# Sliding-window attention in bands on 32-row tiles, its probabilities turned by VectorE, in a two-layer float32 trunk

## The reference, cut to what matters

```python
q, k, v, z = jnp.split(x @ w_in, [SWA_Q, SWA_Q + SWA_KV, SWA_Q + 2 * SWA_KV], axis=-1)
q, k = _rope(q, pos), _rope(k, pos)                 # 16 and 2 heads of 64
s = jnp.einsum("bnqhgd,bnkhd->bnhgqk", qb, kb).astype(f32) * HD ** -0.5   # blocks of 128 queries, 256 keys
rel = qi + W - kj
valid = (rel >= 0) & (rel < W) & (blk * W + kj - W >= 0)
s = jnp.where(valid[None, :, None, None], s, -jnp.inf)
p = jax.nn.softmax(jnp.concatenate([s, sink], axis=-1), axis=-1)[..., :-1]
o = jnp.einsum("bnhgqk,bnkhd->bnqhgd", p.astype(vb.dtype), vb).reshape(bsz, t_len, SWA_Q)
return (o * jax.nn.silu(z)) @ w_out
```

## Time and profile before

| | |
|---|---|
| median of 3 runs | 1020.15 us (1019.94 to 1022.01) |
| the profiled execution | 1020.63 us |
| its span, first to last instruction | 1018.9 us |
| its mean granted TensorE clock | 0.998 of full speed |
| the stage of the change, first to last gate group but one | 768.85 to 909.99 us of the span |

### The profile page before, as it was taken

One profiled execution on the slowest core, in us unless ns is written; L12 is line 12 of the kernel. 1 busy time (PEld: TensorE's weight loads), 2 busy tenths in 40 slices (PEclk: granted clock), 3 DMA queues, 4 the chain that ended last, 5 costly groups with the idle time before them and its releaser, 6 DMA issues.

```text
span 1018.9 us, 17445 instructions
## 1 busy us (share of the span) xinstructions
PE 993.9 (98%) x6318; PEld 813.1 (80%) x6318; DVE 675.4 (66%) x1296; ACT 462.2 (45%) x1349; POOL 291.7 (29%) x647
## 2 busy tenths in 40 slices
PE   7999999999999999999999999999999999999997
PEld 6888787888788787888888888888787777776885
DVE  4677768586867676754456766533447888788655
ACT  4655466575756666644355111302126545556000
POOL 1008483828474746563000000000102222221000
PEclk9999999999999999999999999999999999999999
DMA  6232414133241324234113212302000010014211
GB/s 211 64 104 68 119 42 110 52 67 96 42 120 37 114 47 106 55 87 115 42 41 144 85 42 65 102 11 73 1 21 22 22 43 21 23 63 115 93 42 62
DMA packets 89974, 71.04 MB, mean 70 GB/s; under 512 B 32768, under 2 KB 79008, under 8 KB 89888
## 3 DMA queue, kind: packets, MB, share of 16 engines
q1 hardware_dynamic: 55568, 53.07, 17.4%
q10 hardware_dynamic: 34320, 16.84, 6.6%
HBM read 59.38 MB, written 10.52 MB: 69 GB/s over the span
## 4 chain that ended last, share of the span: by engine, by line
PE 82%; DVE 7%; ACT 6%; DMA 3%; issue 2%; ACTq 0%; DVEq 0%
PE ps L741 28%; PE ps L928 14%; PE ps L1000 9%; PE ps L1105 8%; PE ps L1130 3%; PE ps L941 2%; PE ps L1089 2%; DVE tok L1524 2%; PE ps L1117 2%; PE ps L898 1%; PE ps L909 1%; DMA ws_raw<-in_b_w_in 1%; PE ps L907 1%; PE ps L818 1%; PE ps L886 1%
## 5 line engine op out<-in xcount | busy, mean ns | idle before, releaser
L741 PE MATMUL ps<-act_hi,w_hi 128*128 128x512 f32 x512 | 223.6, 437 | 0.2 <-DVE w_lo L1475 0.2
L741 PE MATMUL ps<-act_hi,w_lo 128*128 128x512 f32 x512 | 201.1, 393 | 0.0
L741 PE MATMUL ps<-act_lo,w_hi 128*128 128x512 f32 x512 | 200.2, 391 | 0.0
L1524 DVE SCALAR_TENSOR_TENSOR tok<-xs,convw,tok 128x512 f32<-128x512 f32 x144 | 115.9, 805 | 15.5 <-ACT xs L1236 13.7
L672 POOL TENSOR_TENSOR rank<-inverse,tok 128x60 f32<-128x60 f32 (+24 forms) x248 | 98.2, 396 | 96.2 <-DMA tok<-blocks_in 78.0
L741 PEld LDWEIGHTS ps<-act_hi,w_lo 128*128 128x128 f32 x512 | 96.1, 188 | 21.2
L741 PEld LDWEIGHTS ps<-act_hi,w_hi 128*128 128x128 f32 x512 | 97.0, 189 | 12.2 <-issue 0.4
L741 PEld LDWEIGHTS ps<-act_lo,w_hi 128*128 128x128 f32 x512 | 97.2, 190 | 10.0
L675 POOL TENSOR_TENSOR inverse<-inverse,rank 128x60 f32<-128x60 f32 (+24 forms) x248 | 97.5, 393 | 19.4
L928 PE MATMUL ps<-wo_hi,act_hi 128*128 128x512 f32 x224 | 88.4, 395 | 1.0 <-DVE wo_lo L1627 1.0
L928 PE MATMUL ps<-wo_lo,act_hi 128*128 128x512 f32 x224 | 87.5, 391 | 0.0
(11 more groups left out here) (273 smaller groups left out, 2187.0 us busy)
## 6 DMA issues: line engine op xcount, KB each, us to landing
w_raw<-in_a_w_in ACTq DMA_DIRECT2D x32, 512.0 KB, 4.3
tok<-in_x SPq DMA_DIRECT2D x8, 512.0 KB, 7.1
decay<-gc_rows SPq DMA_DIRECT2D x8, 512.0 KB, 5.5
tok<-blocks_in SPq DMA_DIRECT2D x32, 128.0 KB, 2.6
v_turn<-v_tok SPq DMA_DIRECT2D x8, 512.0 KB, 6.0
v_tok<-v_turn SPq DMA_DIRECT2D x32, 128.0 KB, 2.9
xres<-in_x SPq DMA_DIRECT2D x8, 512.0 KB, 3.6
ws_raw<-in_b_w_in SPq DMA_DIRECT2D x16, 256.0 KB, 2.7
```

The costliest lines, as they stand in the source:

```text
L741: mm = pe.matmul(ps[:, g % 2, :], lhs[:, k, :], rhs[:, k, HALF * b:HALF * (b + 1)], start=(i == 0), stop=(i == GROUP - 1))
L1524: ins = dve.scalar_tensor_tensor(conv[b], xs[:, b, k:k + HALF], convw[:, k, tile:tile + 1], conv[b], ALU.mult, ALU.add)
```

## The change

A quarter of a block, 32 queries, can see only 159 keys, and these lie in five aligned blocks of 32. The new kernel works on that band (`BAND` = 5, `WIDE` = 160 columns):

- `logits` makes 16 matmuls for each unit, of 160 columns, on eight tiles of 64x32, so that each quarter's queries have their band at column 0. The scale of the logits moves into the copy of the turned queries (L1416).
- The mask touches only the first and the last block of the band (`edges`, 256 elements). The sink is column 161, copied there in every fourth pair; the maximum goes over 161 columns and comes out negated, and the exponentials take the sink along. The operations at L1851, L1854, L1860 and L1429 fall away.
- DVE only inverts the sum (`inverted`). The multiplication by it, over 640 elements, is POOL's, and so is `low_gate`, in every second pair. POOL's selections fall away.
- DVE turns the probabilities by one transpose of 32x32 blocks for each unit (`turned`, 640 elements) straight into `prob`. PE's transposes and ACT's copies of them fall away.
- `values` makes 40 matmuls for each unit (20 in the first block of queries), of 64 columns, on eight tiles of 32x64. Their contraction is over 32 keys, so each quarter needs v in its own 32 partitions: `v_rows`, filled four times over (2 MB) from a copy in DRAM. Three quarters come out in banks 5 to 7, taken by DVE in two operations of 192 elements (`branch`), the fourth in a bank of logits, taken by ACT (`last_rows`).
- The logits of a pair's second unit come a third of a gate group later than the first's.
- At the end of the stage DVE turns the last two units and takes pair 14 ahead of `low_wo(1, 1)`.

```diff
@@ PE
+            def logits(v):
+                k, x, jj, n = unit(v)
+                if k:
+                    pe.wait_ge(s_e, place(k - 1, x) + 1)
+                if k >= 2 and v % 2:
+                    pe.wait_ge(s_ob3, k - 1)
+                for b in range(2):
+                    for a in range(4):
+                        at = n * P + 32 * a
+                        for e in range(2):
+                            r = 64 * e
+                            mm = pe.matmul(ps[32 * a:32 * a + 32, 1 + 2 * x + e, 256 * b:256 * b + WIDE],
+                                           bT[r:r + 64, 2 * jj + b, at:at + 32], kd[r:r + 64, jj // 2, at:at + WIDE],
+                                           start=True, stop=True)
                 mm.then_inc(s_s, 1)
...
+            def values(v):
+                k, x, jj, n = unit(v)
                 kv = jj // 2
...
+                pe.wait_ge(s_pt, v + 1)
+                if v == 0:
+                    pe.wait_ge(s_vr, 64)
+                if v % 2 == 0:
+                    pe.wait_ge(s_e, min(v + 3, UNITS))
+                    if k:
+                        pe.wait_ge(s_ob, 2 * k)
+                for i in range(BAND):
+                    for a in range(4):
+                        row = 4 * (n - 1) + a + i
+                        if row < 0:
+                            continue
+                        bank = last_rows_bank(k) if a == 3 else VALUE_BANK + a
+                        for e in range(2):
+                            mm = pe.matmul(ps[64 * e:64 * e + 64, bank, 64 * x:64 * x + 64],
+                                           v_rows[32 * a:32 * a + 32, row, 64 * kv:64 * kv + 64],
+                                           prob[32 * a:32 * a + 32, x, i, 2 * e:2 * e + 2, :].rearrange("p h q -> p (h q)"),
+                                           start=(i == 0 or row == 0), stop=(i == BAND - 1))
...
             for k in range(PAIRS - 1):
-                turn_probs(2 * k)
-                turn_probs(2 * k + 1)
-                for third in range(3):
-                    project_gate(k + 1, third)
+                project_gate(k + 1, 0)
+                logits(2 * k + 3)
+                project_gate(k + 1, 1)
+                project_gate(k + 1, 2)
                 values(2 * k)
                 values(2 * k + 1)
                 if k + 2 < PAIRS:
                     logits(2 * k + 4)
-                    logits(2 * k + 5)
...
+            pe.wait_ge(s_e, UNITS)
+            pe.wait_ge(s_ob3, PAIRS - 1)
             out_step(1, 0, 0)
-            pe.wait_ge(s_e, UNITS)
             out_step(1, 1, 0)
             values(UNITS - 2)
@@ POOL
+            for v in range(UNITS):
+                k, x, jj, n = unit(v)
+                probs = logit[k % 2][x][:, :, 0:WIDE]
+                pool.wait_ge(s_rden, v + 1)
+                pool.tensor_tensor(probs, probs, sm["rden"][:, k % 2, x, :].unsqueeze(2).broadcast_to([P, 4, WIDE]),
+                                   ALU.mult).then_inc(s_norm, 1)
+                if v % 4 == 0 and v // 4 + 1 < NK:
+                    low_gate(v // 4 + 1)
@@ SP
+            sp.wait_ge(q_val, NT)
+            sp.dma_start(v_rows_out.rearrange("t p d -> p t d"), vv[:, :, :]).then_inc(s_vd, 16)
             for j in range(NK):
                 if j:
                     sp.wait_ge(z_los, j)
+                if j == 2:
+                    sp.wait_ge(s_vd, 16)
+                    sp.wait_ge(q_group, 3 * NT)
+                    for a in range(4):
+                        sp.dma_start(v_rows[32 * a:32 * a + 32, :, :],
+                                     v_rows_out.rearrange("t (b i) d -> i (t b) d", b=4)).then_inc(s_vr, 16)
                 sp.dma_start(z_raw[:, :, :], wb_tiles[:, :, SWA_Z0 + P * j:SWA_Z0 + P * (j + 1)]).then_inc(z_rawd, 16)
@@ DVE
             for k in range(PAIRS - 1):
                 biased(2 * k + 2)
                 biased(2 * k + 3)
-                normalized(2 * k + 2)
-                if k % 2 == 0 and k // 2 + 1 < NK:
-                    low_gate(k // 2 + 1)
-                normalized(2 * k + 3)
+                if k:
+                    branch(k - 1)
+                turned(2 * k)
+                turned(2 * k + 1)
+                inverted(2 * k + 2)
                 if k >= 4 and k % 4 < 2:
                     apply_gate(k // 4 * 2 - 2 + k % 4)
+                inverted(2 * k + 3)
                 if k == PAIRS - 2:
                     low_out(1, 0)
+                    dve.wait_ge(s_pt, UNITS - 2)
                     low_wo(1, 0)
                 gate(k + 1)
-                branch(k)
-            dve.wait_ge(s_pt, UNITS - 2)
+            turned(UNITS - 2)
+            turned(UNITS - 1)
+            branch(PAIRS - 2)
+            dve.wait_ge(s_pt, UNITS)
             low_wo(1, 1)
             low_out(1, 1)
             branch(PAIRS - 1)
```

More of the change, by code:

```diff
@@ L55 @@
 TOKEN_BANKS = (0, 1, 6, 7)
-LOGIT_BANKS = (1, 3)
-GATE_BANK, VALUE_BANK, PROB_BANK = 0, 5, 6
-TURN_BANKS = [2 + n % 2 for n in range(3 * NT - 3)] + [VALUE_BANK, VALUE_BANK, PROB_BANK]
+BAND = 5
+WIDE = 32 * BAND
+GATE_BANK, VALUE_BANK = 0, 5
+TURN_BANKS = [2 + n % 2 for n in range(3 * NT - 3)] + [5, 5, 6]
 PAIRS = UNITS // 2
@@ L114, with unit, place, last_rows_bank @@
 OUT_SLOT = ((0, 1, 2, 0, 1, 0, 1, 3), (0, 1, 2, 0, 1, 2, 0, 1))
+def unit(v):
+    k = v // 2
+    x = (k + v) % 2
+    return k, x, k // 4, 2 * (k % 4) + x
+def place(k, x):
+    return 2 * k + (k + x) % 2
+def last_rows_bank(k):
+    return 4 if k == PAIRS - 1 else 1 + 2 * ((k + 1) % 2)
 def last_use(i, k):
@@ L298, in hybrid_trunk @@
         zt = sbuf(stz, "zt", [P, HALF])
[L299 to L302, removed]
+        room0 = sbuf(stz, "room0", [P, 16])
+        v_rows = sbuf(stz, "v_rows", [P, 4 * NT, P])
+        prob = sbuf(stz, "prob", [P, 2, BAND, 4, 32])
+        logit = [[None, None], [None, None]]
+        logit[1][0] = sbuf(stz, "logit10", [P, 4, WIDE + 1])
+        sm = {n: sbuf(stz, "sm_" + n, [P, 2, 2, 4]) for n in ("neg", "sum", "rden")}
         room1 = sbuf(stz, "room1", [P, (raw_at - 512 - 12 * DM - taken[0]) // 4])
@@ L701, in _, with low_gate @@
                 .then_inc(z_los, 1)
[L703 to L710, removed]
+            def low_gate(j):
+                pool.wait_ge(z_his, j + 1)
+                if j >= 2:
+                    pool.wait_ge(z_group, 2 * (j - 1))
+                pool.tensor_tensor(z_lo[j % 2][:, :, :], z_raw[:, :, :], z_hi[j % 2][:, :, :].bitcast(F32),
+                                   ALU.subtract).then_inc(z_los, 1)
+            for v in range(UNITS):
[6 more added lines that the diff above has]
+                    low_gate(v // 4 + 1)
         @block.tensor
@@ L1071, in _ @@
                 turn_tokens(n - 2)
[L1072 to L1091, removed]
+            pe.wait_ge(q_c, 17)
+            def logits(v):
[12 more added lines that the diff above has]
+                                           start=True, stop=True)
                 mm.then_inc(s_s, 1)
@@ L1297, in high_wo @@
                     act.wait_ge(s_group, 2 * TILES)
+                elif k == 1 and i == 1:
+                    act.wait_ge(z_t, PAIRS)
                 elif k == 2 and i == 1:
@@ L1458, in _ @@
                 tanh_gate(k + 1)
+                last_rows(k)
                 if k % 2 and (k + 3) // 2 < NK:
@@ L1857, in normalized @@
-            def normalized(u):
-                q = u % 2
-                dve.wait_ge(s_e, u + 1)
-                own.next(dve.tensor_tensor(sm["den"][:, q, :], sm["sum"][:, q, :], sm["sink"][:, q, :], ALU.add))
-                own.wait()
-                own.next(dve.reciprocal(sm["rden"][:, q, :], sm["den"][:, q, :]))
-                own.wait()
-                dve.tensor_tensor(logit[u % 4], logit[u % 4],
-                                  sm["rden"][:, q, :].unsqueeze(2).broadcast_to([P, 4, P]), ALU.mult).then_inc(s_norm, 1)
+                dve.tensor_reduce(sm["neg"][:, k % 2, x, :], keys[:, :, 0:WIDE + 1], mybir.AxisListType.X, ALU.max,
+                                  negate=True).then_inc(s_neg, 1)
@@ new lines, in inverted, with turned @@
+            def inverted(v):
+                k, x, jj, n = unit(v)
+                dve.wait_ge(s_e, v + 1)
+                dve.reciprocal(sm["rden"][:, k % 2, x, :], sm["sum"][:, k % 2, x, :]).then_inc(s_rden, 1)
+            def turned(v):
+                k, x, jj, n = unit(v)
+                dve.wait_ge(s_norm, v + 1)
+                if k:
+                    dve.wait_ge(s_pv, 2 * k)
+                dve.transpose(prob[:, x].rearrange("p c h q -> p h c q"),
+                              logit[k % 2][x][:, :, 0:WIDE].rearrange("p h (c i) -> p h c i", i=32)).then_inc(s_pt, 1)
```

169 lines of the change are left out of this document (72 added, 97 removed).

## The result

The changed kernel takes 1034.27 us (median of 4 runs, 1032.68 to 1034.79) against 1021.08 for the kernel before in the same session (1019.94 to 1022.21): a ratio of 1.0127, 95% interval 1.0108 to 1.0145. It is slower by 13 us; I had said faster by 10. The profiled execution took 1032.68 us, with a span of 1030.9 that answers to the 1018.9 of the earlier trace rows.

What follows compares the result with a forecast made beforehand. PE's own instructions were taken to bound the stage. Terms of -21.3 (pairs), +2.7, -0.4, +5.8, +2 and +1.5 gave -9.7 us from a median of 1020.15: forecast 1010, range 1005 to 1014.

Steps and rivals of the forecast that it cites:

- Values, "I take 1.2": PE's values matmuls in each pair: 160 records on eight tiles take 1.2 us, between bounds of 1.16 and 1.76.
- Rival two: PE's pace held by record count, 0.011 us each: values 1.76 a pair, +8 us, 1014 to 1018; chance 0.16.
- The wait for v_rows, +5.8 and +2: Ahead of the first values PE waits for the 2 MB, +5.8 us (4 to 12); lower clock afterwards, +2.
- `apply_gate`, +2.7: In six pairs with this DVE operation, PE waits 0.45 us each for late `z_t`: +2.7 us, at worst 8.2.
- The head, -0.4: Before the second gate group: without a DVE multiplication of 0.69, PE starts at 768.4, -0.4 us.
- The end, +1.5, "0 to 4": Behind the last gate group: PE saves 1.0 us and may wait 0 to 4 us, net +1.5.
- The slow rival: Small-tile records start at least 25 ns apart, or row tiles don't run side by side: +42 us, 1052; chance 0.08.
- rival three: DVE and POOL become the bound in the pairs: 1016 by `apply_gate`, 1035 by slower POOL operations; chance 0.14.
- my 8.64: PE's time for a full pair, gate, values, logits and passages between tile shapes: 8.64 us in place of 10.01.

Runs made afterwards that it cites:

- half-columns run: Changed kernel with each values matmul from the second pair on taking 32 columns instead of 64, record count unchanged: 1032.97 us, ratio 1.0110.
- the order alone: Changed kernel, DVE's first low parts ahead of the last reciprocals, ACT's first output weight's high part between the last two units' exponentials: 1030.91 us.

## Why the prediction was wrong

In one thing it was right: through the 14 pairs the chain runs on PE alone, and no other engine's work becomes the bound. The steps that failed are two terms of the sum for PE, and the term for the end.

- **Values, "I take 1.2".** They measured 1.74 without the passage, +0.54 a pair (+0.45 with a first block), 7.2 us over the pairs. I had the limit in the earlier trace rows, 0.011 a record, and called it no limit, since three tiles took no longer than two. That argument was wrong: a pace that is just enough looks the same as one that is ample. The half-columns run shows it. Rival two had this size.
- **Gaps, in none of my cases.** 5.5 us over the pairs and 3.7 behind them. I had looked at each instruction's execution and never at its supply. The change takes a pair's PE instructions from (24 + 8 + 16 + 32) x 2 = 160 to about 500 in less time. The Trainium skill ("Runtime: NRT & Kernel Launch", section "Instruction fetch mechanics") says that instructions are loaded in blocks of 16 KiB, 256 of them, the next while the current one is executed, and calls the cost mostly hidden. The blocks agree with the trace, in the count of packets and in the places of the gaps; the cost here was not hidden, at 0.2 to 2.5 us a time. Pairs with a gap also take 0.16 to 0.49 more than its idle time, against pairs of 9.24 (8.86 with a first block) without one: another 2.3 over the eight.
- **The wait for v_rows, +5.8 and +2.** The mechanism was right, the sizes were 8.26 and 1.26. From the first issue to the first values it took 12.4 where I had put 9.5: the loads ran at about 200 GB/s, half the rate that I had reckoned with.
- **`apply_gate`, +2.7.** It cost nothing: the chain never passes through DVE in these pairs. DVE's durations were right (0.43, 0.83, 0.35, 0.82 for 0.41, 0.87, 0.33, 0.77), POOL's multiplication took 1.45 for 1.36.
- **The head, -0.4.** It measured -0.37.
- **The end, +1.5, "0 to 4".** It measured +8.2. Two gaps are 3.7 of it. The rest is a chain that I hadn't followed through: the last unit's logits inside the last gate group make its exponentials late, these hold up ACT's high part, one of DVE's low parts runs into POOL's multiplication and takes twice as long, and the first output step starts 13.2 after the group's start where it was 8.8, at a granted clock of 0.61 (of 927 to 931). Undoing the place of the logits gives 5.7 back; the order alone gives 3.4 in the medians, which is not clear of the scatter.
- **The slow rival**, by the rule of the Trainium skill ("TensorE: Matmul & The Clock Gate", section "Wait — 56ns, not 53.3ns?"), about 25 ns between starts: the trace disagrees. Records on eight tiles start 11 ns apart. The 1035 of rival three lies near the measured time by chance, for DVE and POOL never bound the pairs.

The forecast for the span was -9.7 and it measured +12.0, 21.7 apart. Of this the values are 7.2, the gaps in the pairs with what goes with them 5.5 + 2.3 = 7.8, the end 8.2 - 1.5 = 6.7, the wait and its clock 9.5 - 7.8 = 1.7, and gate and logits 0.8 (a full pair without a gap takes 9.24, of which values explain 0.54 over my 8.64); `apply_gate` gives 2.7 back. That is 21.5. Against my -9.7 only the gaps, 7.8 + 3.7 = 11.5 with those behind the pairs, are large enough to turn the sign by themselves; by this sum the kernel without them would have been level with the one before, not 10 faster.

## What to carry to other kernels

Before splitting matmuls onto more and smaller tiles, count records and instructions besides columns: here 160 records of 64 columns took 1.89 us where 80 of 128 took 1.43, with the same columns on each tile. Look for the fastest pace in the trace and take it as a limit unless a row beats it. Where a change triples the instructions of a stretch on one engine, give the loading of instructions a term of its own; and where a weave of two stages ends, follow the last item through every engine, for the loop's slack isn't there any more.

## What I had not expected of the hardware

- A wait on PE for a semaphore that has long been reached isn't free: six instructions of this kind between matmuls put these 0.66 us apart instead of 0.233, 0.106 each.
- PE stopped for 0.2 to 2.5 us at every 256th instruction of its stream where it used them up quickly, and went on 1.2 to 1.6 after the 16 KB packet had landed. No row of the chain names this; the count of q8 packets and the places of the stops do.
- Four loads of 512 KB, each in pieces of 512 bytes to 32 partitions, side by side, filled the DMA engines at about 200 GB/s, where the earlier trace rows have 404. The small pieces alone don't explain it: a load of `z_raw`, to 128 partitions in pieces of 512 bytes too, reached 300 to 360 in the middle of its flight. No run separates the causes.
- On DVE a subtraction of 1024 elements from SBUF takes 2.28 us when it begins under POOL's multiplication, and 1.2 without.
